# Expert blocks in a new order of turns, and first output tiles in pairs

## The reference

```python
# first block, each layer
h = rmsnorm(x, g_attn[layer]) * (1.0 + scale1) + shift1
x = x + gate1 * mixer_layer(h, w_in[layer], w_out[layer], ...)
h = rmsnorm(x, g_mlp[layer]) * (1.0 + scale2) + shift2
up = h @ w_up[layer]                     # 1024 -> 2 * 2816
...
# second block, at its end
y = routed_experts(ht, expert_idx, combine_w, w_gate, w_up, w_down)
#   1024 (token, expert) slots, padded for each expert to blocks of 128 rows;
#   a block: (silu(xb @ w_gate[e]) * (xb @ w_up[e])) @ w_down[e]
#   w_gate, w_up: 1024 x 512, w_down: 512 x 1024, for each of 32 experts
```

## Time and profile before

| | us |
|---|---|
| median of three runs | 2940.51 |
| the profiled execution | 2939.78 |
| its span, first to last instruction | 2938.0 |
| PE busy | 2530.9 (86%) |
| DVE busy | 1151.2 (39%) |
| ACT busy | 727.4 (25%) |
| chain that ended last: PE / DMA / DVE | 67% / 11% / 10% |

### The profile page before, as it was taken

One profiled execution on the slowest core, in us unless ns is written; L12 is line 12 of the kernel. 1 busy time (PEld: TensorE's weight loads), 2 busy tenths in 40 slices (PEclk: granted clock), 3 DMA queues, 4 the chain that ended last, 5 costly groups with the idle time before them and its releaser, 6 DMA issues.

```text
span 2938.0 us, 31205 instructions
## 1 busy us (share of the span) xinstructions
PE 2530.9 (86%) x10789; PEld 1547.6 (53%) x10790; DVE 1151.2 (39%) x2421; ACT 727.4 (25%) x1399; POOL 87.8 (3%) x92
## 2 busy tenths in 40 slices
PE   2899988999988999889999988979998468877884
PEld 2556543888875565448888733637445233333331
DVE  6556653444524546435445233330122332222223
ACT  1101551322312015513223215320122121111112
POOL 0000000000000000000000000000000211111110
PEclk7999698999998997989999989999998779999997
DMA  6656002323343530013232302103223068899996
GB/s 221 165 169 207 15 1 57 93 87 101 101 124 89 160 111 16 15 44 101 82 108 91 122 29 65 65 21 123 72 86 121 11 271 355 356 389 386 371 378 257
DMA packets 248788, 413.77 MB, mean 141 GB/s; under 512 B 20762, under 2 KB 224065, under 8 KB 236225
## 3 DMA queue, kind: packets, MB, share of 16 engines
q1 hardware_dynamic: 232945, 398.25, 39.2%
q0 software_dynamic: 11552, 8.47, 0.9%
q10 hardware_dynamic: 4144, 5.15, 0.5%
HBM read 419.64 MB, written 24.67 MB: 151 GB/s over the span
## 4 chain that ended last, share of the span: by engine, by line
PE 67%; DMA 11%; DVE 10%; issue 7%; ACT 4%; SPq 1%; POOL 0%; ACTq 0%; DVEq 0%; PEld 0%; POOLq 0%; PEldq 0%
PE bank L517 19%; DMA arena<-in_expert_up_w 9%; PE bank L531 8%; PE bank L533 8%; PE bank L532 8%; PE bank L845 4%; PE bank L523 4%; DVE toep L1255 3%; PE bank L854 3%; PE bank L509 2%; PE bank L573 2%; PE bank L563 2%; PE bank L552 2%; PE bank L846 1%; DVE rs L1347 1%
## 5 line engine op out<-in xcount | busy, mean ns | idle before, releaser
L517 PE MATMUL bank<-hT,arena 128*128 128x512 f32 x1408 | 640.2, 615 | 59.1 <-issue 18.1
L517 PEld LDWEIGHTS bank<-hT,arena 128*128 128x128 f32 x1408 | 276.7, 198 | 414.2 <-issue 392.8
L845 PE MATMUL bank<-arena,xT 128*64 128x512 f32 x560 | 286.0, 671 | 87.9 <-DMA arena<-in_expert_up_w 82.4
L846 PE MATMUL bank<-arena,xT 128*64 128x512 f32 x560 | 286.5, 672 | 0.0
L533 PE MATMUL bank<-hT_r,arena_r 128*128 128x512 f32 x704 | 278.7, 396 | 0.0
L845 PEld LDWEIGHTS bank<-arena,xT 128*64 128x64 f32 x560 | 83.4, 154 | 246.2 <-issue 242.6
L532 PE MATMUL bank<-arena_r,S_r 128*128 128x512 f32 x528 | 210.5, 399 | 0.0
L1666 DVE TENSOR_TENSOR S<-S,bank 64x512 f32<-64x512 f32 x78 | 53.4, 685 | 399.9 <-ACT S L1208 328.9
L1255 DVE SCALAR_TENSOR_TENSOR toep<-arena,small,toep 128x256 f32<-128x256 f32 x336 | 162.9, 485 | 12.0
L531 PE MATMUL bank<-hT_r,S_r 128*128 128x512 f32 x352 | 144.5, 410 | 21.3 <-DVE arena_r L1255 21.3
L523 PEld LDWEIGHTS bank<-arena,hT 128*128 128x128 f32 x1280 | 150.6, 198 | 7.8 <-issue 7.8
(11 more groups left out here) (330 smaller groups left out, 3421.2 us busy)
## 6 DMA issues: line engine op xcount, KB each, us to landing
arena<-in_expert_gate_w SPq DMA_DIRECT2D x32, 2048.0 KB, 13.6
arena<-in_expert_up_w SPq DMA_DIRECT2D x32, 2048.0 KB, 18.3
arena<-in_expert_down_w SPq DMA_DIRECT2D x32, 2048.0 KB, 9.0
arena<-in_w_mod SPq DMA_DIRECT2D x48, 1024.0 KB, 6.3
arena<-in_w_up SPq DMA_DIRECT2D x88, 512.0 KB, 4.6
arena<-in_w_in SPq DMA_DIRECT2D x68, 512.0 KB, 5.9
arena<-in_w_down SPq DMA_DIRECT2D x40, 512.0 KB, 4.1
arena<-in_w_out SPq DMA_DIRECT2D x24, 512.0 KB, 4.0
```

What stands on the lines that cost most here:

```text
L517: ins = mm(b[:, 0:width], w[:, k, j * P:(j + 1) * P], src[:, k, 0:width], start=k == 0, stop=k == KD - 1)
L845: mm(bank[half][gate0:gate0 + SUB, :], x, expert_weights(par, 0)[:, k, :], start=k == 0, stop=k == KD - 1)
L846: ins = mm(bank[half][up0:up0 + SUB, :], x, expert_weights(par, 1)[:, k, :], start=k == 0, stop=k == KD - 1)
```

## The change

Nothing in the attention routines is edited; they already handle heads in pairs in both kernels. What is edited:

1. **Turns.** There are 8 spare blocks and 40 turns, in four groups of ten: experts 0, 1, 2 of a group, a spare, experts 3 to 6, a spare, expert 7 (`TURN`). The row tables are looked up through `COLUMN`.
2. **Slots.** The slot set is given by the expert's own parity, and a spare block uses the set of the expert before it. A load waits for the last block that used its slots, so behind a spare it waits for the spare's turn too.
3. **Order of loads.** Gate and up of block b+1 are issued before down of block b.
4. **First tiles.** `feature_pair` makes both tiles of the first slot together: for each k it waits for the chunk once and does j = 0 and j = 1. In the MLP's first pair the loops over j and k are exchanged.

```diff
-OVER = 7
-FIRST = 2
+OVER = 8
+TURN = (0, 1, 2, None, 3, 4, 5, 6, None, 7)
...
+            def load_turn(g, q, parts):
+                g, q = g + q // TURNS, q % TURNS
+                if TURN[q] is None:
+                    o = g * len(SPARE) + SPARE[q]
+                    e = sp.value_load(blkE[0:1, bass.ds(o, 1)], min_val=0, max_val=EXPERTS - 1)
+                    has_rows = sp.value_load(blkU[0:1, bass.ds(o, 1)], min_val=0, max_val=1)
+                    with sp.If(has_rows > 0):
+                        for m in parts:
+                            for half in range(2):
+                                sp.wait_ge(s[f"in{half}_done" if m < 2 else f"down{half}_done"], g * TURNS + q)
+                            load_part(e, TURN[q - 1] % 2, m, f"w_o{m}")
+                else:
+                    e, slot = g * 8 + TURN[q], TURN[q] % 2
+                    was = q - 1
+                    while TURN[was] is None or TURN[was] % 2 != slot:
+                        if TURN[was] is None and TURN[was - 1] % 2 == slot:
+                            break
+                        was -= 1
+                    for m in parts:
+                        for half in range(2):
+                            sp.wait_ge(s[f"in{half}_done" if m < 2 else f"down{half}_done"], g * TURNS + (was + 1))
+                        load_part(e, slot, m, f"w_e{3 * slot + m}")
...
-            for o in range(OVER):
-                b = FIRST + o
...
-                with sp.If(has_rows > 0):
-                    for m in range(3):
-                        slots_free(b, m)
-                        load_part(e, b % 2, m, "w_o")
-            with sp.Fori(0, (EXPERTS - FIRST) // 2) as g:
-                for par in (1, 0):
-                    b, e = g * 2 + (FIRST + OVER + 1 - par), g * 2 + (FIRST + 1 - par)
-                    for m in range(3):
-                        slots_free(b, m)
-                        load_part(e, par, m, "w_e")
+            load_turn(0, 2, (0, 1))
+            with sp.Fori(0, BLOCKS // TURNS - 1) as g:
+                for q in range(3, TURNS + 3):
+                    load_turn(g, q, (0, 1))
+                    load_turn(g, q - 1, (2,))
...
+            def feature_pair(banks, w, src, arrived):
+                for k in range(KD):
+                    pe.wait_ge(s["h_ready"], arrived + (k + 1))
+                    for j in range(2):
+                        ins = mm(banks[j][:, :], w[:, k, j * P:(j + 1) * P], src[:, k, :], start=k == 0, stop=k == KD - 1)
+                        if k == KD - 1:
+                            ins.then_inc(s["tiles_done"], 1)
...
-                        for j in range(2):
-                            for k in range(KD):
-                                at = (k % 4) * QUARTER + j * P
...
+                        for j, k in [(j, k) for k in range(KD) for j in range(2)] if f == 0 else [(j, k) for j in range(2) for k in range(KD)]:
...
+            def expert_turn(g, q, first=False, last=False):
+                b = g * TURNS + q
+                expert_in(g, q)
+                turn_act(b - 1)
+                if not last:
+                    turn_rows((q + 1) % 2, g * (TURNS // 2) + (q + 1) // 2)
+                expert_out(g, q - 1, first)
```

More of the change, by code:

```diff
@@ L420, in _, with load_part @@
             ew = [a["expert_gate_w_2"][0], a["expert_up_w_2"][0], a["expert_down_w_2"][0]]
[L422 to L431, removed]
+            def load_part(e, slot, m, told):
+                w = ew[m][bass.ds(e, 1)].rearrange("e (p k) n -> p (e k) n", k=KD if m < 2 else 4)
+                dst = ering[:, 3 * (1 - slot) + m, :].rearrange("p (k n) -> p k n", k=w.shape[1])
+                sp.dma_start(dst, w).then_inc(s[told], 16)
@@ L859, in second_half @@
                 with pe.If(flag > 0):
-                    work(par, 1)
+                    work(par, slot, 1)
                 with pe.Else():
                     pe.sem_inc(s[done], 1)
[L864 to L869, removed]
-                    pe.wait_ge(s["act_e"], b * 2)
[L871 to L874, removed]
@@ L884, in expert_out @@
[L884 to L893, removed]
-                    for m in range(2):
-                        pe.wait_ge(s[f"w_o{3 * par + m}"], 16 * (o // 2 + 1))
-                    gate_up(par, 0)
-                    gate_up(par, 1)
-                with pe.Else():
-                    pe.sem_inc(s["in0_done"], 1)
-                    pe.sem_inc(s["in1_done"], 1)
@@ new lines, in expert_out @@
+                    with pe.Else():
+                        pe.sem_inc(s["down0_done"], 1)
+                        pe.sem_inc(s["down1_done"], 1)
+                else:
+                    e, slot = g * 8 + TURN[q], TURN[q] % 2
+                    more = pe.value_load(blkM[0:1, bass.ds(e, 1)], min_val=0, max_val=1)
+                    pe.wait_ge(s["actT_ready"], b + 1)
+                    if not first:
+                        for half in range(2):
+                            pe.wait_ge(s[f"y{half}_ready"], b * 2)
+                    pe.wait_ge(s[f"w_e{3 * slot + 2}"], g * 64 + (16 * (TURN[q] // 2) + 16))
+                    down(par, slot, 0)
+                    second_half(more, down, par, slot, "down1_done")
@@ L947, in _ @@
-            expert_in(b, 0, EXPERTS - 1, n)
-            turn_act(b - 1)
-            expert_out(b - 1, 1, EXPERTS - 2, n)
-            turn_act(b)
-            expert_out(b, 0, EXPERTS - 1, n)
+            expert_turn(0, 1, True)
+            with pe.Fori(0, BLOCKS // TURNS - 1) as g:
+                for q in range(2, TURNS + 2):
+                    expert_turn(g, q)
+            for q in range(2, TURNS):
+                expert_turn(BLOCKS // TURNS - 1, q, last=q == TURNS - 1)
+            turn_act(BLOCKS - 1)
@@ L1228, in _ @@
             copy_out(1, 1, None)
[L1229 removed]
+            with act.Fori(1, BLOCKS // 2 - 1) as g:
                 for par in range(2):
```

178 lines of the change are left out of this document (87 added, 91 removed).

## The result

The changed kernel takes 2868.9 us (median of 4 runs, 2863.56 to 2872.79), the kernel before beside it 2939.0 (4 runs): a ratio of 0.9759, 95% interval 0.9744 to 0.9774. It is faster by 70 us; 2857 was forecast.

A forecast was written before the change was run, and what follows sets the result against it. Expert stage taken as DMA-bound, TensorE not far behind: 2938.0 less 72.8 (experts) and 11 (first tiles) gives a 2854.2 span; adding 1.8 and 0.7 gives a 2857 us median, range 2832 to 2905.

The forecast's parts named there:

- Early start, continuous loads: Expert stage: expert 2's gate and up issued at 2315.6 instead of 2360.6, DMA running through from 2333.8.
- The price of a turn, 16.4: Expert stage: DMA-bound turn falls from 17.1 to 16.4 us, 29 turns making 475.6 us.
- the full-share end of the bounds: Expert turn at full DMA share: 16.1 us; as a rival with 2 us start loss, 2838, chance 0.10.
- The rival of an unchanged rate: Expert loads: new order brings no better rate, turn stays 17.1 us, 20 us more, 2877; chance 0.20.
- The start loss of 12 us: Early expert turns: close second halves with a spare beside them overrun the slots' slack; 12 us, between 2 and 20.
- the rival of the exposed spare turns: Expert stage: PE doesn't catch up, each of eight spares costs 6.8 us for gathers, 54 us, 2911; chance 0.14.
- PE's 125 us a group: Expert stage: ten turns need 125 us of PE against 131 us of DMA, so loads cover the spares.
- The turn of 14.4 us: Expert stage: PE's own time for one expert turn without the wait for up weights, 14.4 us.
- The end, 43.8: From expert 31's first pass to the span's end: 43.8 us instead of 46.8, one down pass falling away.
- Gathers behind the backlog: Expert stage rival: gathers land behind all weights issued, two turns take 32.8 us, 2976, slower than before; chance 0.06.
- First tiles, 11: MLP first pairs of both layers: second tile done beside the first gains 11 us, from 0 to 12; projections 0.
- The feared low clock: MLP first pair: PE's clock may stay at 1.2 GHz, the 48 matmuls needing 25 us, no gain.

The follow-up runs named there:

- e6: Kernel before with loads of experts 2 and 3 issued ahead of the spare turns, loads of spare blocks left out; 2940.85 us, ratio 0.9999.
- e5: Changed kernel with each gather of rows issued ahead of the scatter of the turn before instead of behind it; 2854.38 us, ratio 0.9713 to the kernel before.
- e11: e5 with half of each down weight's load left out from expert 2 on; 2812.97 us, ratio 0.9575 to the kernel before.
- e7: Kernel before with the new order of loads, spare turns at their old places; 2899.02 us, ratio 0.9858.
- e1: Kernel before with only the five loop exchanges of the first tiles; 2933.49 us, ratio 0.9958.
- e8: e5 with gate and up of expert 3 issued before down of expert 2; 2854.65 us, ratio 0.9715 to the kernel before.
- e3: Changed kernel with the loops of the first tiles put back; 2877.89 us, ratio 0.9777 to the kernel before.
- e9: Changed kernel with half of each down weight's load left out from expert 2 on; 2846.79 us, ratio 0.9678 to the kernel before.

## Why the prediction was nearly right, point by point

- **Early start, continuous loads: mechanism right.** Expert 2's loads went out at 2304.88 and its down at 2321.50 (forecast 2333.8 - 10.3 = 2323.5: 2.0 earlier). The start of two loads alone is not where the gain comes from: in e6 it brought nothing.
- **The price of a turn, 16.4: 0.4 too high.** 16.0 was measured, the full-share end of the bounds. The loads are not alone in it: PE waits in that window for gathers and not for weights, and with the gathers out of the way (e5) the loads give 16.2. 29 turns at 256.57 / 16 = 16.04 are 465.0 us, 10.6 less than forecast. The rival of an unchanged rate, 0.20, is out.
- **The start loss of 12 us: the step that was mis-sized.** From 2321.50 to the first pass of expert 31 at 2815.59 are 494.1 us; less 29 x 16.04 = 465.0 that is 29.1 us. In e5, by the same count, 2805.87 - 2321.58 - 29 x 16.24 = 13 us, near the 12 forecast. Where it lies differs from the forecast, though. Of the 29.1, 200.76 - 11 x 16.04 = 24.3 lie before 2522.26, in 11 turns, and 4.7 behind 2778.83; of the 13 in e5, 186.08 - 11 x 16.24 = 7.4 and 5.9. So the second halves cost some 7 us where PE doesn't wait for gathers, less than the 12; some 5 us went in the two turns after that, for which the prediction had no term; and some 16 us came with the gathers, which the prediction had costed at nothing for the whole stage. Its argument, that PE catches up under the loads, was true from 2522 on alone; before that PE was already behind through the second halves. This is a part of the rival of the exposed spare turns: it gave 54 us and cost 13.5. The range took in half of that rival, the sum none of it.
- **PE's 125 us a group: too high,** 112 in e11. The turn of 14.4 us was read where the clock was partly low. Here are the windows of its first pass (to the activation's transposes) and of that of expert 31, both in the kernel before:

```profile
2756.83:2765.54 8.71, 8.71 (x32) 3.09 (x33) 0.00 (x0) 0.00 (x0) 1.44 (x2) 0.80 1.00 423
2891.23:2898.24 7.01, 7.01 (x32) 2.60 (x32) 0.00 (x0) 0.84 (x2) 1.00 (x1) 1.00 0.89 317
```

  The same pass takes 8.7 us at a granted clock of 0.80 and 7.0 at 1.00, and 2822.55 - 2815.59 = 7.0 in the changed kernel. The trace of before could have told. The conclusion (PE fits beside the loads) stood, with more room than I gave it.
- **The end, 43.8: 2.3 too low.** 2861.7 - 2815.59 = 46.1. The pass that falls away did, but the last down pass took 6.43 us against 3.65. In e5, where it took 3.65, the end is 2849.3 - 2805.87 = 43.4. The windows of that pass, in the changed kernel and in e5 (granted clock 0.56, near the level of 1.2 GHz, and 1.00, the level of 2.4 GHz):

```profile
2826.82:2833.20 6.38, 6.38 (x16) 1.72 (x16) 1.38 (x2) 0.00 (x0) 0.98 (x1) 0.56 0.02 3
```

```profile
2817.12:2820.80 3.68, 3.65 (x16) 1.06 (x16) 1.38 (x2) 0.00 (x0) 0.97 (x1) 1.00 0.04 5
```

  What PE did in the 4.2 us before is the same in both; why the clock fell in one of them stays open.
- **Gathers behind the backlog (slower, 0.06): out.** In e7, from 2541 to 2786 us (issues, KB each, median us to landing), a down load landed after 24.2 us, where it took 9.0 in the kernel before, and a gather still after 14.5:

```profile
arena<-in_expert_down_w SPq DMA_DIRECT2D x15, 2048.0 KB, 24.2
...
xT<-h_scratch,src_c POOLq DMA_INDIRECT x15, 14.5
```

  The longer queue of weights didn't delay the gathers (14.5 against 14.6). The Trainium skill's round-robin (DMA: Bandwidth & Descriptors, Queues, rings and completion order) agrees with that; the traces don't show single packets.
- **First tiles, 11: right,** 10.3 in the profile, 12.4 in e1. The feared low clock didn't come: between 505 and 520 us the granted clock was 1.00 in the changed kernel, the level of 2.4 GHz, and 0.67 before, though PE waits within the pair for each chunk.
- **Sum.** 2854.2 + 0.7 (tiles) - 2.0 (start) - 10.6 (rate) + 17.1 (start loss) + 2.3 (end) = 2861.7, the span. Two misses of opposite sign hid each other. The median lies 5.3 above the profiled execution, which was the fastest of the four, and not 0.7; that is two fifths of the miss of 12 us. Over the four runs the time falls as the mean granted clock rises (0.923 at 2863.56, 0.921 at 2872.79), and the same holds among the runs of e1 (0.919 at 2922.55, 0.913 at 2940.64); what moves the clock from run to run no run shows.

What the prediction had wrong in its weights is the split between the parts: it gave 20 us to the order of loads (29 x 0.7) and the rest to the places; the runs say 42 and 21 alone. I had read the 0.85 of the first stretch as the price of the second halves; with the new order they cost little (in e7 the share there is 0.96), where the loads of the next expert no longer stand behind a down pass.

A version that beats both is e5: 2854.38 us, 0.9713 of the kernel before (0.9695 to 0.9730), by one exchange in POOL's queue.

## What to carry to other kernels

Where an engine waits by turns for two things, removing one shows only what the other leaves: cross both before calling one the bound. An in-order queue that holds loads with different release times runs empty behind the latest of them; issue each load at the place where its slot comes free, and look at an indirect DMA's queue in the same way. When work is started earlier, ask which later load follows it: the start that only filled the buffers brought nothing here.

## What was unexpected of the hardware

- Small gathers and large loads share the DMA engines at the gathers' cost: 2.3 us to landing alone, 14.5 to 14.6 beside 2 MB weight loads, whether these land after 9 us or after 24. In e6 the same gathers under early loads held PE once for 12.69 us, in the kernel before for 8.51.
- A DMA share of 0.97 to 0.98 carried 399 to 404 GB/s over 250 us. The kernel before had 381 at 0.94: most of what was to be had was the idle 6%. The rate while busy, an estimate from these rows, is 381 / 0.94 = 405 before and 399 / 0.97 = 411 after.
- The last down pass took 3.65 us in the kernel before, e5, e7 and e8, 5.35 in e3 and e9, 6.17 in e11 and 6.43 in the changed kernel, though its code is the same; in the last its granted clock was 0.56, in e5 1.00.
